# Second mixing stage: dense products spread over the attention's steps, and the recurrence moved between attention heads three and four

## The reference

```python
p = h @ cd_w_in                      # 2848 columns: attention part, recurrence part
oc = native_sparse_attention(...)    # 8 heads in 2 groups; compressed, selected, window branch
od = mlstm(dq, dk, dv, di, df, dog)  # 4 heads of a gated linear recurrence
x  = x + concat([oc, od]) @ cd_w_out
```

## Time and profile before

| | us |
|---|---|
| median of three runs (2753.27 to 2763.5) | 2756.98 |
| the profiled execution | 2771.19 |
| its span | 2769.4 |
| TensorE matmul busy | 2658.4 (96%) |
| TensorE weight loads busy | 2113.3 (76%) |
| VectorE (DVE) busy | 1460.6 (53%) |
| ScalarE (ACT) busy | 985.6 (36%) |
| GpSimd (POOL) busy | 524.8 (19%) |

### The profile page before, as it was taken

One profiled execution on the slowest core, in us unless ns is written; L12 is line 12 of the kernel. 1 busy time (PEld: TensorE's weight loads), 2 busy tenths in 40 slices (PEclk: granted clock), 3 DMA queues, 4 the chain that ended last, 5 costly groups with the idle time before them and its releaser, 6 DMA issues.

```text
span 2769.4 us, 32004 instructions
## 1 busy us (share of the span) xinstructions
PE 2658.4 (96%) x13148; PEld 2113.3 (76%) x13148; DVE 1460.6 (53%) x1903; ACT 985.6 (36%) x1662; POOL 524.8 (19%) x554
## 2 busy tenths in 40 slices
PE   8989998999999998899999999999999988999998
PEld 7777876788888666686788888888878645888887
DVE  8875996644333588646543334433354565434332
ACT  3235644422222533543322223222233445322221
POOL 5711001322200011100222101221002124222200
PEclk9899999999999998899999999999999989999999
DMA  4433112232332231001323332223323300223232
GB/s 153 90 97 109 64 47 69 76 101 97 97 96 93 78 93 44 28 2 61 100 99 99 93 104 92 97 94 95 105 76 122 116 16 1 76 99 99 92 97 86
DMA packets 76931, 232.17 MB, mean 84 GB/s; under 512 B 14961, under 2 KB 16241, under 8 KB 76529
## 3 DMA queue, kind: packets, MB, share of 16 engines
q1 hardware_dynamic: 64176, 212.46, 23.8%
q0 software_dynamic: 4400, 9.71, 1.5%
q10 hardware_dynamic: 8208, 7.96, 0.9%
HBM read 220.13 MB, written 5.77 MB: 82 GB/s over the span
## 4 chain that ended last, share of the span: by engine, by line
PE 78%; DVE 12%; ACT 5%; POOL 2%; issue 1%; DMA 1%; ACTq 0%; DVEq 0%; POOLq 0%
PE ps L358 77%; DVE mem L375 4%; DVE part L445 3%; ACT part L433 1%; DVE mem L388 1%; PE ps L369 1%; POOL mem L3285 0%; POOL mem L398 0%; ACT mem L509 0%; DVE mem L393 0%; DVE mem L408 0%; DVE mem L3040 0%; DVE mem L553 0%; DVE mem L2167 0%; DVE mem L634 0%
## 5 line engine op out<-in xcount | busy, mean ns | idle before, releaser
L358 PE MATMUL ps<-part,part 128*128 128x512 f32 (+2 forms) x9774 | 2248.3, 392 | 33.6 <-DVE part L445 9.5
L358 PEld LDWEIGHTS ps<-part,part 128*128 128x128 f32 (+1 forms) x9774 | 1834.7, 189 | 442.3 <-issue 16.0
L445 DVE TENSOR_TENSOR part<-mem,part 128x1024 fp32r<-128x1024 f32 (+2 forms) x419 | 560.1, 1343 | 595.5 <-ACT part L433 595.1
L433 ACT ACTIVATE part<-mem 128x1024 fp32r<-128x1024 f32 (+2 forms) x419 | 415.8, 1003 | 266.4 <-DMA mem<-in_ffb_down 56.1
L375 DVE TENSOR_TENSOR mem<-ps,mem 128x512 f32<-128x512 f32 (+1 forms) x266 | 176.7, 664 | 298.6 <-PE ps L358 289.5
L358 PE MATMUL ps<-mem 128*64 128x64 f32 (+13 forms) x2568 | 269.5, 313 | 38.3 <-ACT mem L2385 10.3
L358 PEld LDWEIGHTS ps<-mem 128*64 128x64 f32 (+5 forms) x2568 | 183.2, 167 | 112.9 <-issue 44.0
L517 POOL TENSOR_TENSOR mem<-mem 128x512 f32<-128x512 f32 x62 | 80.5, 1299 | 717.9 <-ACT mem L509 716.9
L1669 POOL TENSOR_TENSOR mem<-mem 128x512 f32<-128x512 f32 x88 | 113.8, 1293 | 381.5 <-ACT mem L1657 381.5
L1671 POOL TENSOR_TENSOR part<-mem,part 128x512 fp32r<-128x512 f32 x88 | 113.8, 1293 | 353.0 <-ACT part L1660 353.0
L1660 ACT ACTIVATE part<-mem 128x512 fp32r<-128x512 f32 x88 | 55.6, 632 | 327.8 <-DVE mem L375 327.8
(11 more groups left out here) (192 smaller groups left out, 1169.8 us busy)
## 6 DMA issues: line engine op xcount, KB each, us to landing
mem<-in_ffa_gate SPq DMA_DIRECT2D x44, 512.0 KB, 3.2
mem<-in_ffa_up SPq DMA_DIRECT2D x44, 512.0 KB, 3.3
mem<-in_ffb_gate SPq DMA_DIRECT2D x44, 512.0 KB, 3.3
mem<-in_ffb_up SPq DMA_DIRECT2D x44, 512.0 KB, 3.3
mem<-in_ffa_down SPq DMA_DIRECT2D x32, 512.0 KB, 3.5
mem<-in_ffb_down SPq DMA_DIRECT2D x32, 512.0 KB, 3.5
mem<-in_w_odd SPq DMA_DIRECT2D x24, 512.0 KB, 3.3
mem<-in_w_ab SPq DMA_DIRECT2D x22, 512.0 KB, 3.2
```

The costliest lines, as they stand in the source:

```text
L358: return e.matmul(out, l, r, start=start, stop=stop, skip_group_check=True)
L433: w.e.activation(K.wts[c % NH].h[:, 0:n], K.raws[c % NR][:, 0:n], ACT.Copy).then_inc(*K_A.up(("w", c)))
L445: w.e.tensor_tensor(t.l, K.raws[c % NR][:, 0:n], t.hf, SUB).then_inc(*K.V.up(("w", c)))
```

## The change

- **Order of the weights and of the front.** `blocks` is the stage's first product and the norm's sums follow its first chunk. `gates`, `mconv`, `dv`, `og` leave the front; their chunks come behind those of `cv` and the compression.
- **The attention's first three heads** (24 steps, 27 turns: `nsa_first_tensor` and its counterparts on the other engines) come directly behind the compression. Behind each score TensorE puts in pieces of the dense products, one piece being one k of a chunk, so three matmuls: none in turns 0 to 3, four in turns 4 to 11, then 3, 3, 2 in turn (`MIXED_IN`): gates in turns 4 and 5, `mconv` in 6 to 14, `dv` in 15 to 26 (one token block after the other, so its four chunks are held until the last). All of these accumulate in bank 7. The convolution, the gate rows and the SiLU follow in the same turns on DVE and ACT. The convolution's result and sum share one tile.
- **The recurrence** comes after 24 steps, then the **fourth head** with four pieces of `og` behind each of its eight scores, the norm and division of the recurrence, and at the end sigmoid and the product with the output gate (a multiplication of its own on DVE, two heads at a time).
- **Banks.** Scores, compressed scores, compressed transposes, `F0`, `cT`, the norm's sums and the division's factors take turns in two pairs of banks, 0/1 and 2/3 (`take_pair`). The attention's output has bank 6 alone; the outputs of heads one to three are copied to SBUF by ACT in turns 11 and 19 and after turn 26, and split into `y2` in the last head.
- **Memory.** The attention's tiles move from the area of `h` (which the dense products now still read) to the area of the early tiles; `y2` gets other homes; clearing the convolution's pads on POOL is issued after the rope's turns.

```diff
@@ weight_order
     first[7] = len(out)
-    rows("w_cd", [16])
-    rows("w_cd", range(8, 16))
-    by_token("w_dv", T)
     rows("w_cd", range(6, 8))
...
     by_token("w_cv", 280)
     out += nsa[6:]
+    rows("w_cd", [16])
+    rows("w_cd", range(8, 12))
+    by_token("w_dv", T)
+    rows("w_cd", range(12, 16))
     rows("w_cd_out", range(8))
@@ Kernel
+    def take_pair(self, w, names, emptied_by):
+        first = 2 * (self.turn % 2)
+        self.turn += 1
+        for c, name in enumerate(names):
+            self.take(w, name, emptied_by, bank=first + c)
+        return self.ps[:, first:first + 2, :]
@@ TensorE
+CHUNK = dict(blocks=0, cq=2, cv=14, gates=20, mconv=21, dv=25, og=29, out=33)
+FIRST_HEADS = 24
+MIXED_IN = [0] * 4 + [4] * 8 + [3, 3, 2] * 5
 def cd_tensor(K, w):
...
+    for o in linear(K, w, "blocks", 2, 8, K.h, h_ready, K.V):
+        if o == 0:
+            norm_tensor(K, w, 7, K.ss)
+            norm_columns_tensor(K, w, 7)
...
+    nsa_first_tensor(K, w)
     mlstm_tensor(K, w)
-    nsa_tensor(K, w)
+    nsa_last_tensor(K, w)
+def units_tensor(K, w, name, n):
+    for o in range(n):
+        acc = K.take(w, (name, o), K.V, bank=7)
+        c, ap = next_weights(K, w)
+        for k in range(8):
+            done = mm3(w.e, acc, ap.cols(k * P, P), K.h[k], k == 0, k == 7)
+            if k == 7:
+                done.then_inc(*K.P.up(("w", c), (name, o)))
+            yield
+def nsa_first_tensor(K, w):
+    gates, mconv = units_tensor(K, w, "gates", 1), units_tensor(K, w, "mconv", 4)
+    dv = dv_units_tensor(K, w)
+    for i in range(FIRST_HEADS + 3):
+        if i < FIRST_HEADS:
+            nsa_score_tensor(K, w, i)
+        for _ in range(MIXED_IN[i]):
+            next(gates if i < 6 else mconv if i < 15 else dv)
+        if i == 0:
+            compress_turn_tensor(K, w, 1)
+        elif i < 4:
+            compressed_tensor(K, w, i - 1)
+        nsa_compressed_tensor(K, w, i)
+        if 0 <= i - 2 < FIRST_HEADS:
+            nsa_turn_tensor(K, w, i - 2)
+        if i >= 3:
+            nsa_values_tensor(K, w, i - 3)
...
+def nsa_last_tensor(K, w):
+    og = units_tensor(K, w, "og", 4)
+    for n in range(11):
+        i = FIRST_HEADS + n
+        if n < 8:
+            nsa_score_tensor(K, w, i)
+            for _ in range(4):
+                next(og)
+        if n == 1:
+            mlstm_sums_tensor(K, w)
+        if n in (6, 8):
+            mlstm_factors_tensor(K, w, (n - 6) // 2)
...
@@ DVE
 def cd_vector(K, w):
...
     stt(w, E.cos, K.cc("cos"), 0.125, K.rstd, MUL, MUL)
     stt(w, E.sin, K.cc("sin"), 0.125, K.rstd, MUL, MUL)
     for o in range(2):
-        weights_lo(K, w, c + 13 + o + 3)
+        weights_lo(K, w, c + o + 3)
         w.wait_ge(*K.P["blocks", o])
...
+def nsa_first_vector(K, w):
+    E, c = K.cd, K.first[7]
+    for i in range(FIRST_HEADS + 3):
+        if i < FIRST_HEADS:
+            nsa_max_vector(K, w, i)
+        if 0 <= i - 1 < FIRST_HEADS:
+            nsa_factor_vector(K, w, i - 1)
+        nsa_compressed_vector(K, w, i)
...
+        if i == 5:
+            weights_lo(K, w, c + CHUNK["mconv"] + 3)
+            gates_vector(K, w)
+        if i == 7:
+            weights_lo(K, w, c + CHUNK["mconv"] + 4)
+            mconv_vector(K, w, 0)
+        if i == 8:
+            mlstm_gates_vector(K, w, 0)
+        if i == 9:
+            weights_lo(K, w, c + CHUNK["dv"] + 1)
+            mconv_vector(K, w, 1)
+        if i == 11:
+            mlstm_gates_vector(K, w, 1)
+            weights_lo(K, w, c + CHUNK["dv"] + 2)
+            mconv_vector(K, w, 2)
...
+        if i == 14:
+            mlstm_gates_vector(K, w, 2)
+            mconv_vector(K, w, 3)
@@ ACT
+def nsa_first_scalar(K, w):
+    E, e, c = K.cd, w.e, K.first[7]
+    for i in range(FIRST_HEADS + 3):
+        if i in (11, 19):
+            nsa_kept_scalar(K, w, (i - 11) // 8)
+        if 0 <= i - 2 < FIRST_HEADS:
+            nsa_turned_scalar(K, w, i - 2)
+        if i < FIRST_HEADS:
+            nsa_exp_scalar(K, w, i)
+        nsa_compressed_scalar(K, w, i)
...
+        if i == 6:
+            weights_hi(K, w, c + CHUNK["mconv"] + 4)
+            w.wait_ge(*K.V["gates_d"])
+            act(w, E.sp, E.gr[32:36, :], ACT.Abs)
+            act(w, E.sp, E.sp, ACT.Exp, scale=-1.0)
+            act(w, E.sp, E.sp, ACT.Ln, "softplus", bias=1.0)
...
+        if i == 15:
+            weights_hi(K, w, c + CHUNK["dv"] + 4)
+            for o in range(4):
+                w.wait_ge(*K.V["conved", o])
+                e.activation(E.qk[:, o, :], E.qk[:, o, :], ACT.Silu).then_inc(*K.A.up(("qk", o)))
+        if i in (17, 20, 23, 26):
+            dv_scalar(K, w, (i - 17) // 3)
```

More of the change, by code:

```diff
@@ L2602, in __init__ @@
         m.flat(16 * T)
-        self.y2 = K.pairs(at, at + 8 * T, 8)
-        self.sq = [K.mem[:, at + T * k:at + T * k + T] for k in range(4, 8)]
         self.q = m.tiles(4)
@@ L2730, in compressed_tensor @@
     elif part == 1:
-        acc = K.take(w, ("kcm", 0), K.A, bank=6)
+        acc = K.take(w, ("kcm", 0), K.A, bank=7)
         for g in range(2):
@@ L2788, in mlstm_factors_tensor @@
 def mlstm_factors_tensor(K, w, p):
-    turn = 7 + 3 * p
     w.wait_ge(*K.V["factors"])
+    both = K.take_pair(w, [("F", 2 * p + c) for c in range(2)], K.V)
     for c in range(2):
         hd = 2 * p + c
-        acc = K.take(w, ("F", hd), K.V, bank=2 * (turn % 2) + c)
-        done = mm(w.e, acc, K.cst[0:4, CC["sel"] + P * hd:CC["sel"] + P * hd + P], K.cd.gr[0:4, :], True, True)
+        done = mm(w.e, both[:, c, :], K.cst[0:4, CC["sel"] + P * hd:CC["sel"] + P * hd + P], K.cd.gr[0:4, :], True,
+                  True)
@@ new lines, in nsa_score_tensor, with nsa_turn_tensor @@
+def nsa_score_tensor(K, w, i):
+    E = K.cd
+    hd, br, t = STEPS[i]
+    n = (t + 1) * P
+    both = K.take_pair(w, [("nscore", i, g) for g in range(2)], K.A)
+    for g in range(2):
+        r = slice(64 * g, 64 * g + 64)
+        done = mm(w.e, both[:, g, 0:n], E.q[r, hd, t * P:n], E.kk[r, br, 0:n], True, True)
+    done.then_inc(*K.P.up(("nscore", i)))
+def nsa_turn_tensor(K, w, u):
+    E = K.cd
+    t = STEPS[u][2]
+    for g in range(2):
+        acc = K.take(w, ("npt", u, g), K.A, bank=4 + g)
+        w.wait_ge(*K.G["npr", u, g])
+        for kt in range(t + 1):
+            done = tr(K, w.e, acc[:, kt * P:(kt + 1) * P], E.pr[u % 3][:, g, kt * P:(kt + 1) * P])
+    done.then_inc(*K.P.up(("npt", u)))
```

561 lines of the change are left out of this document (308 added, 253 removed).

## The result

The changed kernel is **slower by 1.4%**: median 2800.05 us of four runs (2795.6 to 2804.89) beside 2760.24 of four runs of the kernel before (2753.27 to 2765.55), ratio 1.0143, 95% interval 1.0118 to 1.0169. The profiled execution took 2804.9 us, its span 2803.1. The forecast was 2764 with a range to 2795.

A forecast was written before the change was run, and what follows sets the result against it. TensorE was taken as nearly full in the attention, with only 3.7 us of pauses per head. Front -66.7 and the later parts +74 gave +7; 2771.2 + 7 - 14.2 = 2764 us, range 2738 to 2795.

The forecast's parts named there:

- no change worth the name: Whole kernel: the forecast's own case, time within 0.5%, 2743 to 2771 us, chance 0.48.
- Front, -66.7: Stage's front: thirteen dense chunks leave, 26.2 instead of 94.4 us, -68.2, with 1.5 back for a lower clock.
- The new pause: Entry of the front: TensorE waits 8 us before compression, where before it was 0.4.
- Start of the attention, 19.6: Steps 0 to 3, without dense work, behind ACT's in-order queue: step 4 begins about 19.6 us after the compression.
- Steps 4 to 26, 124: First three heads: 105.4 us of TensorE's own work at full clock plus 18.8 of waits, 124 us.
- Recurrence, 35.5: Recurrence after 24 steps: row products in 3.5, first sums 9.5 after its beginning, then 26; 35.5 us.
- Last head, 59: Fourth head with output-gate pieces: 49 us of work, plus waits for bank 7, pairs, sigmoids and gated heads; 59 us.
- the denominator's: Last head: a wait of 1.2 us because the denominator holds bank 7.
- the two at the end: Last head: 3.6 us for sigmoids and their load ahead of transposed copies, 2.8 for gated heads' late parts.
- Minus 14.2 for the profile against the median: Whole kernel: the profiled execution, 2771.2 us, lay 14.2 above the median of three runs, 2757.0; subtracted at the end.
- VectorE becomes the bound: Steps 5 to 15: DVE's 56 us against TensorE's 53 might not overlap, +22, about 2786; chance 0.35 for above 2771.
- Room that I don't see: Attention: pair and bank waits don't show, 2745, or about 2735 with clock gains; chance 0.17 for below 2743.

The follow-up runs named there:

- trimmed changed kernel: The changed kernel with 264 of the 312 moved matmuls left out, waits, copies and vector instructions kept: 2763.4 us, ratio 1.0005 to the kernel before.

## Why the prediction was wrong

The forecast was no change worth the name: +7 us, within 0.5%. It came as +40, 1.4%, and 2800 lies above the range. By its steps:

1. **Front, -66.7: right.** 147.5 to 81.0 us is -66.5. The new pause was forecast at 8 us, the row shows 7.08. That the matmuls were busy there for all of the time didn't make them the front's price: left out by themselves they give back 10 us.
2. **Start of the attention, 19.6: right**, 19.8 measured.
3. **Steps 4 to 26, 124: right in sum**, 126.1 measured, the granted clock 0.95 near 1 as forecast. The waits were in the places named, with other sizes: the scores behind a shared pair show 3.5 us of pauses (0.67, 1.96, 0.23, 0.67) against 6.9, bank 7 shows 7.0 against 8.2, the SiLU 4.68 against 2.2. Turning ScalarE's order round took some 6 us off these steps, more than its own pauses, because the SiLU's shrank to 2.94 as well. What the step left out is that the order was a choice: its price was taken as given.
4. **Recurrence, 35.5: failed**, 43.8. The part up to the first sums was forecast at 9.5 us with ScalarE's two high parts in it and took 10.1: the 1.95 pause is that term, and it held. The part behind it was forecast at 26 and took 33.7 (2280.2 to 2313.9). Two things were wrong in it. VectorE's four low parts (2.35 us for two) were priced at nothing; two of them stand ahead of the product behind the 2.12 pause. And 2.5 us were taken off for the half clock at its start, which didn't go: the first sums take 3.23 us as they did in the kernel before (2199.59, 3.23), the clock is 0.50 to 0.62 until 2287, and 0.66 again behind the second pause (2299 to 2304). With the parts in other turns both pauses go, the clock is 1.00 from 2269.7 on, and the recurrence takes 36.4. The term has a slip of its own: 29.17 - 2.5 - 1.7 is 25.0, not 26; the 29.17 row ends before the last group of 1.1 us.
5. **Last head, 59: failed**, 69.1. Of the waits, the two for pairs came as forecast (0.8 and 1.8; the rows show 0.81 and 1.50), the denominator's came as 0.57 for 1.2, and the two at the end, forecast at 3.6 and 2.8, came as 1.07 and 4.42. Two were not in the working. The 3.45 is the row sums' step on VectorE (L403), which waits for a ScalarE square (L3478) that stands behind a transposed copy and two exponentials; the sums share the pairs with the scores, so the next score waits for it:

```profile
2331.75 0.68 DVE L403 SCALAR_TENSOR_TENSOR mem<-ps,mem 4x512 f32<-4x512 f32 x1 [4.81 <-ACT mem L3478]
```

   The 2.25 is bank 7: VectorE has the compressed branch's row work and a reciprocal of 1.73 us ahead of reading out the output gate's chunk. Together the pauses are 14.1 us against 10.2. The larger part is the clock (0.89 over the head), priced at nothing here: three of the eight dense groups (2333.12, 2353.45, 2364.49) took 4.6 us each, and the eight together 28.0 from start to start against the 22.7 forecast. ScalarE's other order took 6.4 us out of the head's steps.
6. **Minus 14.2 for the profile against the median: failed.** It took the surplus of the profiled execution for something that both kernels share. 7.7 us of it lay in this very stage and went with the clock; the changed kernel's first profile is 4.8 us above its median, and its stage has the lower clock in both profiles (0.90 and 0.89). The stage to compare with was nearer 304 than 312. One profile could not tell how large it was; the range should have held it.

Together: recurrence 8.3, last head 10.1, first loop 2.1, the two small ones 0.4, the stage of the kernel before 7.7; that is 28.6 of the 33 us between 2800 - 2760 and the +7. The other 4 are within the spread of executions.

**The rivals.** *VectorE becomes the bound* (2786) came nearest in size, but not as written: VectorE was busy 51.5 of 66.1 us (78%, not over 90%) from step 5's mask to step 16's, and the longest pauses there name ScalarE's exponential, not a convolution. There is something in it: the parts and the vector and table work cost 12.7 + 8.5 us of time in the attention, and where an edit put a convolution ahead of the rows' copy, the next score waited 4.14 us. *Room that I don't see* was wrong. By the Trainium skill, Perfetto Trace Analysis, "Identifying the Most-Contended Engine", the weight loads gave an estimate of 47 us of room. The runs don't agree: 60.1 us of dense matmuls placed behind the scores cost 37, so at most 23 were covered. That the granted clock would give back more than I had in mind was half true: steps 4 to 26 did run at 0.95, but the lower level came back in the recurrence (0.81) and in the last head (0.89), where pauses remained.

The table loads stayed at 1.28 us with the next activation right behind them, as in the forecast. No pause of TensorE in the stage names a transfer; the moved chunks' DMA (share 0.10 instead of 0.03) cost nothing that shows, as forecast.

Open: when a pause is followed by half clock and when not; what the front could give in another order of its queues; and the last 5.5 us of the difference.

## What to carry to other kernels

Before moving matmuls out of a stretch, ask what the stretch costs without them: take them away in both places and time it. A busy engine can be busy over work that another chain would make as long. And when dense pieces go between a producer and its consumer, go through every in-order queue that serves the step: an order that was right (copy, then exponential) can turn wrong, and a high or low part that lands ahead of a product for which TensorE waits costs its own time and can cost more through the clock. Compare with more than one profile of the kernel before when a stretch runs at two clock levels.

## What the runs showed of the hardware that was not expected

What a wait can cost through the clock: the same six matmuls took 3.23 us behind a pause of 1.95 and 1.97 behind one of 0.21, and twelve dense ones 4.62 instead of 3.02 behind one of 2.25. But behind the same pause of 1.96 us twelve dense matmuls took 3.02 in one profile of the changed kernel and 4.45 in the other, so the price isn't fixed. The same instructions of one stage took 304.1 or 311.8 us in two profiles of one kernel, with a granted clock of 0.95 or 0.92; in its recurrence the clock differed too (0.92 and 0.84) and the time did not. And with TensorE work taken out, what stays ran at a lower clock (0.79 instead of 0.89 in the trimmed changed kernel, 0.61 instead of 1.00 in the front of the kernel before), so that removing 60 us returned 37 and 10.
